# Tiles that are added stand twice in DRAM, and the raw load leaves out two tiles

## The reference

```python
def swiglu_2(x, w_gate, w_up, w_down):
    return (jax.nn.silu(x @ w_gate) * (x @ w_up)) @ w_down

for l in range(DEPTH_2):                       # DEPTH_2 = 2
    x = layer_norm(ALPHA * x + 0.5 * swiglu_2(x, ffn1_gate[l], ffn1_up[l], ffn1_down[l]), ln_g[l, 0], ln_b[l, 0])
    ...                                        # mixer
    x = layer_norm(ALPHA * x + 0.5 * swiglu_2(x, ffn2_gate[l], ffn2_up[l], ffn2_down[l]), ln_g[l, 2], ln_b[l, 2])
```

## Time and profile before

| | |
|---|---|
| time, median of 3 runs | 2883.94 us (2883.45 to 2889.08) |
| the profiled execution's own time | 2882.77 us |
| its span, first to last instruction | 2881.0 us |
| busy: PE, PEld, DVE, ACT, POOL | 97%, 85%, 59%, 40%, 23% |
| granted PE clock, mean | 0.998 |
| chain that ended last: PE, DVE, DMA, "issue" | 73%, 8%, 7%, 7% |
| of it, DMA `praw<-weight_pairs` | 7% |
| bytes moved, mean rate | 347.03 MB, 120 GB/s |
| paired stages (line 591, first start to last start) | 1003.1 to 1217.0, 1577.2 to 1793.4, 1948.6 to 2166.2, 2526.7 to 2741.2 us |

### The profile page before, as it was taken

One profiled execution on the slowest core, in us unless ns is written; L12 is line 12 of the kernel. 1 busy time (PEld: TensorE's weight loads), 2 busy tenths in 40 slices (PEclk: granted clock), 3 DMA queues, 4 the chain that ended last, 5 costly groups with the idle time before them and its releaser, 6 DMA issues.

```text
span 2881.0 us, 42204 instructions
## 1 busy us (share of the span) xinstructions
PE 2805.8 (97%) x17509; PEld 2443.2 (85%) x17509; DVE 1709.5 (59%) x2357; ACT 1165.8 (40%) x1577; POOL 662.2 (23%) x657
## 2 busy tenths in 40 slices
PE   9999999899999999999999999999999999999999
PEld 8888887678888899988877999888998888889987
DVE  5554443553342587844647878448885465788853
ACT  5232244642232354433345444335433343454432
POOL 0115616101110322210225222122221013422210
PEclk9999999999999999999999999999999999999999
DMA  4332223123222378622213776237772221277722
GB/s 149 96 101 95 90 78 91 55 80 101 95 95 97 112 194 200 169 93 88 82 66 100 197 196 167 95 105 182 197 183 95 87 84 65 96 182 200 183 95 81
DMA packets 144206, 347.03 MB, mean 120 GB/s; under 512 B 17360, under 2 KB 58448, under 8 KB 144016
## 3 DMA queue, kind: packets, MB, share of 16 engines
q1 hardware_dynamic: 100496, 302.39, 31.8%
q0 software_dynamic: 43520, 41.95, 9.8%
HBM read 341.01 MB, written 2.10 MB: 119 GB/s over the span
## 4 chain that ended last, share of the span: by engine, by line
PE 73%; DVE 8%; DMA 7%; issue 7%; ACT 3%; POOL 2%; SPq 0%; DVEq 0%; ACTq 0%; POOLq 0%
PE bank L399 16%; PE bank L401 16%; PE bank L400 16%; DMA praw<-weight_pairs 7%; PE bank L587 4%; PE bank L591 4%; PE bank L589 4%; PE bank L536 2%; PE bank L465 1%; PE bank L469 1%; PE bank L466 1%; PE bank L416 1%; PE bank L422 1%; PE bank L417 1%; ACT phi L1032 1%
## 5 line engine op out<-in xcount | busy, mean ns | idle before, releaser
L1632 DVE TENSOR_TENSOR wlo<-wraw,whi 128x1024 fp32r<-128x1024 f32 x311 | 402.5, 1305 | 440.8 <-ACT whi L1013 440.7
L1013 ACT ACTIVATE whi<-wraw 128x1024 fp32r<-128x1024 f32 x319 | 332.5, 1055 | 478.0 <-DMA wraw<-weights 477.7
L399 PE MATMUL bank<-Ah,whi 128*128 128x512 f32 x1056 | 412.9, 391 | 0.0
L401 PE MATMUL bank<-Al,whi 128*128 128x512 f32 x1056 | 411.0, 389 | 0.0
L400 PE MATMUL bank<-Ah,wlo 128*128 128x512 f32 x1056 | 410.9, 389 | 0.0
L399 PE MATMUL bank<-H,whi 128*128 128x512 f32 x984 | 386.7, 393 | 4.5 <-DVE H L1755 2.1
L401 PE MATMUL bank<-H,whi 128*128 128x512 f32 x984 | 383.2, 389 | 0.0
L400 PE MATMUL bank<-H,wlo 128*128 128x512 f32 x984 | 383.1, 389 | 0.0
L587 PE MATMUL bank<-TF,plo 128*128 128x256 f32 x1280 | 366.3, 286 | 8.9 <-DVE cb L1718 3.2
L589 PE MATMUL bank<-TF,phi 128*128 128x256 f32 x1280 | 362.0, 283 | 0.0
L591 PE MATMUL bank<-TF,phi 128*128 128x256 f32 x1280 | 361.9, 283 | 0.0
(11 more groups left out here) (352 smaller groups left out, 5047.7 us busy)
## 6 DMA issues: line engine op xcount, KB each, us to landing
wraw<-weights SPq DMA_DIRECT2D x319, 512.0 KB, 3.5
praw<-weight_pairs SPq DMA_DIRECT2D x160, 512.0 KB, 4.3
praw<-weight_pairs SPq DMA_DIRECT2D x160, 256.0 KB, 3.0
praw<-weight_pairs POOLq DMA_DIRECT2D x160, 256.0 KB, 4.9
X<-x_t SPq DMA_DIRECT2D x8, 256.0 KB, 7.1
y_t<-X SPq DMA_DIRECT2D x8, 256.0 KB, 2.1
dist<-attention SPq DMA_DIRECT2D x4, 256.0 KB, 4.1
wraw<-weights SPq DMA_DIRECT2D x2, 256.0 KB, 4.3
```

The source lines that it names most:

```text
L399: pe.matmul(b, sh, mh, start=start, stop=False)
L401: signal(pe.matmul(b, sh, ml, start=False, stop=stop), keys)
L1013: act.activation(whi[:, u % NS, :], wraw[:, u % NS, :], ACT.Copy).then_inc(*S.done("weights_hi", ("hi", u)))
L1632: dve.tensor_tensor(wlo[:, u % NS, :], wraw[:, u % NS, :], f32(whi[:, u % NS, :]), SUB).then_inc(*S.done("weights_lo", ("lo", u)))
```

## The change

`pair_plan` now lists ten tiles a unit: (2k+1, j+1), (2k, j), (2k+1, j), and (2k, j+1) twice. The raw load takes the first six tiles of a row into tiles 2 to 7 of the buffer (384 KB), the base the first four into tiles 8 to 11, and the add takes the last four, which is (2k, j+1) twice, in one contiguous piece of 2 KB a row. The tensor grows from 8 to 10 tiles a unit. What is computed stays the same.

```diff
                 for k in range(4):
-                    for kk, jj in ((2 * k, j + 1), (2 * k + 1, j + 1), (2 * k, j), (2 * k + 1, j)):
+                    for kk, jj in ((2 * k + 1, j + 1), (2 * k, j), (2 * k + 1, j), (2 * k, j + 1), (2 * k, j + 1)):
                         plan.extend((f"{m}{n}_{l}", kk, jj) for m in ("gate", "up"))
...
             pool.wait_ge(pair_again[raw], 16 * pair_landings(v))
-            pool.dma_start(praw[raw][:, 8:12, :].rearrange("p (f e) n -> p f (e n)", f=2),
-                           pair_d[v, :, 0:2 * P].unsqueeze(1).to_broadcast([P, 2, 2 * P]), accum_op=ADD).then_inc(
+            pool.dma_start(praw[raw][:, 8:12, :].rearrange("p t n -> p (t n)"), pair_d[v, :, 6 * P:10 * P], accum_op=ADD).then_inc(
                 pair_added[raw], 16)
...
-                sp.dma_start(praw[raw][:, 8:12, :].rearrange("p t n -> p (t n)"), pair_d[v, :, 2 * P:6 * P]).then_inc(
+                sp.dma_start(praw[raw][:, 8:12, :].rearrange("p t n -> p (t n)"), pair_d[v, :, 0:4 * P]).then_inc(
                     pair_again[raw], 16)
-                sp.dma_start(praw[raw][:, 0:8, :].rearrange("p t n -> p (t n)"), pair_d[v]).then_inc(pair_in[raw], 16)
+                sp.dma_start(praw[raw][:, 2:8, :].rearrange("p t n -> p (t n)"), pair_d[v, :, 0:6 * P]).then_inc(
+                    pair_in[raw], 16)
...
-    pairs2 = np.empty((len(plan) // 8, P, 8, P), np.float32)
+    pairs2 = np.empty((len(plan) // 10, P, 10, P), np.float32)
     for i, (name, k, n) in enumerate(plan):
-        pairs2[i // 8, :, i % 8, :] = mats[name][k, n]
-    pairs2 = pairs2.reshape(len(plan) // 8, P, 8 * P)
+        pairs2[i // 10, :, i % 10, :] = mats[name][k, n]
+    pairs2 = pairs2.reshape(len(plan) // 10, P, 10 * P)
```

## The result

| | before | after |
|---|---|---|
| time, median | 2885.09 us (4 runs, 2883.45 to 2889.08) | 2850.78 us (4 runs, 2850.36 to 2854.89) |
| ratio after/before | | 0.9882, 95% interval 0.9865 to 0.9899 |
| profiled execution | 2882.77 us | 2854.89 us |
| paired stages, first to last start of their matmuls, sum of four | 863.3 us | 834.2 us |

The change saves 34.3 us by the medians, against 31 forecast. The profiled execution happens to be the slowest of the four after, which lies ahead of the paired stages: their first matmul starts at 1005.7 us and not at 1002.9, in code that is the same in both.

A forecast was written before the change was run, and what follows sets the result against it. TensorE, 97% busy, was held in the paired stages by adds running one at a time. Of 50.2 us of waits, 15.5 would stay; 34.7 less 10% gives 31 off 2882.8, so 2852 us, range 2846 to 2873.

The forecast's parts named there:

- The adds as pace: Paired stages: adds run one at a time, 4.9 and 0.35 us each, 21.0 us per four, setting the pace.
- The add's cost: POOL's add with one 2 KB piece a row: 4.4 us, the middle of 3.9 to 4.9, instead of 4.9.
- "It matters little" whether there is room: Scratch room for two adds hardly matters: one at a time, four 4.4 us adds need 19.0 us of 20.6.
- The raw load: Raw load of 384 KB instead of 512 lands 0.6 us sooner, in about 3.7 us.
- A few periods, mostly at a stage's start: Raw loads landing after a group's last unit has begun: few periods, 10% left for them, cutting 34.7 us to 31.
- ACT's order as the next holder: ACT runs line 1032 behind 1026 and 1174, leaving PE a 0.43 us wait per period, 15.5 us in all.
- The sum: Line 587's waits: 50.2 us now, 15.5 after, 34.7 saved at most; 31 taken, giving 2852 us.
- Rival 1: The add is no faster and still alone; only the raw load counts, 4 to 8 us, about 2877; chance 0.10.
- Rival 2: Long accumulating pieces are slow, 0.35 us each, adds 1.1 us longer: about 3040 us; chance 0.06.
- Rival 3: More than forecast: the full 34.7 us, 2848, with every raw load in time; chance 0.02 below 2847.

The follow-up runs named there:

- before, scratch 2048: Kernel before the change, with 2048 bytes of descriptor scratch instead of 1024 and nothing else changed: 2870.55 us, ratio 0.9946.
- add only: Kernel before with only the add changed to one contiguous 2 KB piece a row, twelve tiles a unit, raw load still 512 KB: 2860.96 us, ratio 0.9918.
- raw load only: Kernel before with only the raw load cut to six tiles, 384 KB; the add keeps two 1 KB pieces a row: 2874.83 us, ratio 0.9964.
- second profile: Profile of a repeat run of the unmodified changed kernel: profiled execution 2851.1 us, median 2850.72 us, ratio 0.9883 to the kernel before.

## Why the prediction was right

*The adds as pace.* Held. The row of adds is gone, and with it 51 of the 54 waits of DVE. It is shown from both sides: the scratch alone ends the row in the old kernel, and brings it back in the new one. Two figures of the prediction were rough: the gap between a landing and the next start is 0.32 us and not 0.35, and from start to start an add in the row took 5.46 us on average, which makes 21.8 a group and not 21.0. The median of 4.9 us hid that, and it mattered below.

*The add's cost.* 4.4 us taken, 4.3 measured, inside 3.9 to 4.9. Some of that is luck: 4.4 was the middle of two bounds, and it is met only by adds that are free; in a row they take 4.8. The pieces themselves got no quicker, their share of the engines is unchanged, 9.8%. Shorter is POOL's issue, 0.87 us instead of 1.21. Where both kinds of add are free ("before, scratch 2048" and "add only"), the first piece comes 1.93 us after POOL's start with the old pieces and 1.59 with the new, which is that same 0.34. The page "DMA: Bandwidth & Descriptors" of the Trainium skill, section "Anatomy of one DMA", says "You can emit a lot of descriptors before the incremental cost shows up"; here half the pieces took 0.34 us off POOL's instruction. The measurement decides; the page's formula would give 2.6 us for each, an estimate that lies far below both.

*"It matters little" whether there is room.* Wrong. I had counted 4.4 us for adds in a row; in a row they take 4.8, at the very limit that the prediction names, and since the mean counts and not the median (5.28 us from start to start), four don't fit in the 20.6 us. Room is worth 9.3 of the 34 us. The step failed since it took one landing time for adds in a row and free ones.

*The raw load.* The landing was wrong in sign. 3.7 us was predicted; it is 3.7 as long as the adds stay in a row (raw load only), but 4.7 after the full change. The adds are now issued as soon as their base has landed, and more of their pieces fall into the flight of the next unit's loads (1.37 us an engine during a base, 0.40 before). So ACT waits for the raw load 141.3 us and not less than 55.3. "A few periods, mostly at a stage's start" was too few: at 15 of the 36 group ends ACT was still waiting for it, and PE lost 0.71 us there, 0.48 at the others. The sum hides this: waits of 22.3 and 21.8 us were measured in the two profiles, where 15.5 and 3.5 had been counted. The load is still worth its 10 us: 9.9 alone, and 10.2 from "add only" to the full change.

*ACT's order as the next holder.* Held: 0.43 us predicted, 0.39 measured in the group shown, with line 1032 right behind line 1174. Moving that one call took 16.9 us more.

*The sum.* 31 us off a profiled 2882.8, 2852 us; measured 2850.78. That it is so near is partly luck. All 31 us were to come out of the waits of line 587; these fell by 27.1 us (50.2 to 23.1). The stages as a whole got 29.1 us shorter (29.8 in the second profile), and 2 us more came off the stretches between them, for which the prediction has no term. *Rival 1* fell by its time, 2850.78 and not 2877. But one half of it stands: in a row the new add lands no sooner than the old one by the median, and the full gain needed the room as well. *Rival 2* fell: a piece of 2 KB took 0.215 us, not 0.35. *Rival 3* set its floor on the same wait; it would have needed every raw load in time.

## What to carry to other kernels

An engine that idles on "issue" in front of a DMA that it issues itself may be waiting for room for that DMA's descriptors: compare each issue with the landing of the one before. More scratch or fewer, longer pieces both end it; here the longer pieces gave 9.6 us more than the scratch alone. When transfers follow each other in a row, reckon with their mean time, not the median. Then look for the next holder in the written order of the waiting engines: a call that doesn't need anything late should stand ahead of those that do, but that pays only once the transfer in front of it is in time (16.9 us after this change, nothing before it).

## What the runs showed of the hardware

- Pieces of an accumulating DMA cost by their bytes: 16 of 1 KB and 8 of 2 KB an engine take the same 9.8% of the DMA engines, 0.109 and 0.215 us a piece. POOL's instruction doesn't: 1.21 us for the former, 0.87 for the latter.
- With 1024 bytes of scratch two adds of 16 pieces an engine were never under way together, with 2048 bytes they were in 75 of 156 cases; adds of 8 pieces were with 1024 bytes (41 of 156), and never with 320.
- Adds that were blocked for room started 0.31 to 0.32 us behind their predecessor's landing, 143 times in the kernel before, and the profile shows that as idle on "issue", with no releaser.
- Landing times depend on what else is under way more than on the bytes: the raw load of 384 KB takes 3.7 us while the adds stand in a row, 4.7 with adds that follow their base at once, 3.6 ahead of the base.
